# Two query blocks per TensorE step in the paired heads of block 1, and rounded products for the latents' sums of squares

## The reference

```
# block 1, per layer: differential attention (4 heads with two maps each) and
# dilated windows (8 heads of 64), causal, softmax over up to 512 keys
p = softmax(s); pd = p[:, :, 0] - lam * p[:, :, 1]; out = einsum(pd, v)
...
# block 2, per layer: sliding window, latent, stick-breaking and gated heads; the latent ones:
q = (_rmsnorm(cq, g_q) @ w_uq); kv = (_rmsnorm(ckv, g_kv) @ w_ukv)
```

## Time and profile before

| | |
|---|---|
| median of 3 runs | 2328.06 us (2327.0 to 2328.45) |
| the profiled execution's own time | 2326.94 us |
| its span, first to last instruction | 2325.2 us |
| TensorE busy | 2311.6 us (99%) |
| chain of work that ended last | 97% TensorE |
| granted TensorE clock | 0.999 of full speed |

### The profile page before, as it was taken

How to read it: one execution, slowest core, us unless ns; L and a number is a source line. 1 busy time by engine, 2 the same in 40 slices (tenths; PEclk the granted TensorE clock), 3 DMA queues, 4 the chain that set the end, 5 groups by cost and what they waited for, 6 DMA issues and landing times.

```text
span 2325.2 us, 30164 instructions
## 1 busy us (share of the span) xinstructions
PE 2311.6 (99%) x11444; PEld 1880.9 (81%) x11444; DVE 1478.5 (64%) x2773; ACT 981.3 (42%) x1825; POOL 0.2 (0%) x4
## 2 busy tenths in 40 slices
PE   9999999999999999999999999999999999999998
PEld 7888888888888888888877788888887768888887
DVE  6788764345578774344577668566566767668565
ACT  5356542223446653222567533133236664323222
POOL 0000000000000000000000000000000000000000
PEclk9999999999999999999999999999999999999999
DMA  5333333332343333333221232314303112422322
GB/s 176 106 107 105 99 104 91 100 95 96 91 116 105 105 93 116 100 98 111 65 87 55 64 129 91 127 59 140 126 29 97 55 46 100 145 82 90 130 70 91
DMA packets 73583, 226.32 MB, mean 97 GB/s; under 512 B 14240, under 2 KB 15136, under 8 KB 72672
## 3 DMA queue, kind: packets, MB, share of 16 engines
q1 hardware_dynamic: 73296, 224.13, 30.9%
q10 hardware_dynamic: 144, 0.26, 0.0%
HBM read 204.83 MB, written 2.10 MB: 89 GB/s over the span
## 4 chain that ended last, share of the span: by engine, by line
PE 97%; DVE 1%; ACT 1%; DMA 0%; issue 0%; DVEq 0%; SPq 0%
PE bank L585 26%; PE bank L587 25%; PE bank L586 25%; PE bank L2196 2%; PE bank L2194 2%; PE bank L2195 2%; PE bank L1279 2%; PE bank L2009 1%; PE bank L1968 1%; PE bank L1266 1%; PE bank L1993 1%; PE bank L519 1%; PE bank L1256 1%; PE bank L1254 1%; PE bank L2022 1%; PE bank L2051 0%
## 5 line engine op out<-in xcount | busy, mean ns | idle before, releaser
L585 PE MATMUL bank<-h_hi,w_hi 128*128 128x512 f32 x1984 | 788.1, 397 | 0.7 <-DVE w_lo L1125 0.2
L587 PE MATMUL bank<-h_lo,w_hi 128*128 128x512 f32 x1984 | 774.0, 390 | 0.0
L586 PE MATMUL bank<-h_hi,w_lo 128*128 128x512 f32 x1984 | 773.7, 390 | 0.0
L585 PEld LDWEIGHTS bank<-h_hi,w_hi 128*128 128x128 f32 x1984 | 372.9, 188 | 83.1 <-issue 10.4
L1125 DVE TENSOR_TENSOR w_lo<-raw_w,w_hi 128x1024 fp32r<-128x1024 f32 x314 | 379.1, 1222 | 93.1 <-ACT w_hi L1113 89.9
L587 PEld LDWEIGHTS bank<-h_lo,w_hi 128*128 128x128 f32 x1984 | 372.5, 188 | 79.3
L586 PEld LDWEIGHTS bank<-h_hi,w_lo 128*128 128x128 f32 x1984 | 373.2, 188 | 72.7 <-issue 1.2
L1113 ACT ACTIVATE w_hi<-raw_w 128x1024 fp32r<-128x1024 f32 x314 | 327.7, 1054 | 145.5 <-DMA raw_w<-w_dram 145.2
L2429 ACT ACTIVATE nrm<-bank 128x512 f32<-128x512 f32 x44 | 26.4, 599 | 289.5 <-PE bank L587 289.5
L1568 ACT ACTIVATE ext<-bank 128x512 f32<-128x512 f32 x48 | 28.7, 599 | 279.7 <-PE bank L587 279.7
L1868 DVE TENSOR_TENSOR rope_a<-ext,bank 128x512 f32<-128x512 f32 x32 | 22.0, 688 | 160.9 <-PE bank L587 107.4
(11 more groups left out here) (369 smaller groups left out, 3506.4 us busy)
## 6 DMA issues: line engine op xcount, KB each, us to landing
raw_w<-w_dram SPq DMA_DIRECT2D x312, 512.0 KB, 3.6
down_raw<-w_dram SPq DMA_DIRECT2D x36, 512.0 KB, 4.4
extra_raw<-w_dram SPq DMA_DIRECT2D x10, 512.0 KB, 4.5
k_lo<-k_lo SPq DMA_DIRECT2D x32, 128.0 KB, 2.4
ln_row<-row_dram SPq DMA_DIRECT2D x4, 1024.0 KB, 6.8
last_raw<-w_dram SPq DMA_DIRECT2D x8, 512.0 KB, 4.5
x<-x_dram SPq DMA_DIRECT2D x4, 512.0 KB, 6.4
rowp<-row_dram SPq DMA_DIRECT2D x2, 1024.0 KB, 9.8
```

What stands on the lines that cost most here:

```text
L585: nc.tensor.matmul(dst, lh, rh, start=start, stop=False)
L586: nc.tensor.matmul(dst, ll, rh, start=False, stop=False)
L587: return nc.tensor.matmul(dst, lh, rl, start=False, stop=stop)
```

## The change

- In the paired heads 4, 5 and 6 of block 1 (`JOINED1`) query blocks 0 and 1 are one TensorE step: their scores are issued together, into columns 0 to 127 and 128 to 383 of the two banks (`columns1`); then come the interlude of the steps before and the fills of both blocks. Their transposes and their weighted values are issued together too, one group and two groups later. ScalarE copies the transposed weights of both blocks at once (384 columns per map). VectorE and ScalarE still treat their softmax block by block.
- The read-out of the head before moves from qb 1 to qb 2 in joined heads, also the square of an output on ScalarE.
- In all heads the values' transposes go from qb 3 to qb 2 and the sum of squares from qb 2 to qb 3; the split of the squares goes from qb 1 to qb 2; the differential heads' epilogue goes behind the normalisation of qb 0.
- In block 2 the squares of both latents are split by VectorE into a high and a low part (`split_latent`), and TensorE sums them with two rounded products.
- In step 5 of block 2 ScalarE copies `kr` out ahead of the exponentials instead of behind them.

The diff's core (left out: the same change of columns, `columns1` for 0 to (qb+1) x 128, in `scores`, `pv`, `softmax_exp`, `row_max` and `normalise`, the waits that go with it, counts, and the removed lines of the old loop of TensorE, which is printed above):

```diff
+latent_sq = {"cq": (sq_lo, sb("cq_sq_lo", [P, SEQ], F32R, at=addr["sz0"])),
+             "ckv": (sq_lo, sb("ckv_sq_lo", [P, SEQ], F32R, at=addr["z_t"]))}
...
     if a < LAST:
-        LATE1[a, 3] = ("v", a + 1)
+        LATE1[a, 2] = ("v", a + 1)
     if 1 <= a <= N_A:
-        LATE1[a, 2] = ("sum", a - 1)
+        LATE1[a, 3] = ("sum", a - 1)
...
+JOINED1 = range(N_A, LAST)
+GROUPS1 = []
+for a in range(N_ATT):
+    GROUPS1 += [((a, 0), (a, 1))] if a in JOINED1 else [((a, 0),), ((a, 1),)]
+    GROUPS1 += [((a, 2),), ((a, 3),)]
+GROUP1_AT = {group[0]: i for i, group in enumerate(GROUPS1)}
+def second1(a, qb):
+    return qb == 1 and a in JOINED1
+def last1(a, qb):
+    return (a, 1) if qb == 0 and a in JOINED1 else (a, qb)
+def columns1(a, qb):
+    return slice(P, 3 * P) if second1(a, qb) else slice(0, (qb + 1) * P)
...
     def transposes(a, qb):
         pe.wait_ge(probs_normed, at(probs_normed, 4 * a + qb + 1))
         for m in range(1 if a < N_A else 2):
-            i = ti1(a, qb, m)
-            if i >= 2:
+            i, own = ti1(a, qb, m), columns1(a, qb)
+            to = own.start if a >= N_A else 0
+            if i >= 2 and not (a >= N_A and second1(a, qb)):
                 pe.wait_ge(t_out, at(t_out, i - 1))
             for b in range(qb + 1):
-                last = nc.tensor.transpose(T[i % 2][:, b * P:(b + 1) * P], pn[m][:, b * P:(b + 1) * P], ident)
+                last = nc.tensor.transpose(T[i % 2][:, to + b * P:to + (b + 1) * P],
+                                           pn[m][:, own.start + b * P:own.start + (b + 1) * P], ident)
             last.then_inc(t_ready, 1)
...
+    def late(a, qb):
+        use, f = LATE1.get((a, qb), (None, 0))
+        if use == "v":
+            v_transpose(f)
+        elif use == "sum":
+            sum_squares(f)
+    for i, group in enumerate(GROUPS1):
+        a, qb = group[0]
+        if qb == 0 and a in (0, LAST):
+            fill(a, qb, 0)
+        if banks1(a, qb) is S:
+            for own in group:
+                scores(*own)
+        if (a, qb) == (LAST, NB - 2):
+            scores(a, qb + 1)
+        if qb or a not in (0, LAST):
+            fill(a, qb, 0)
+        if i >= 2:
+            for own in GROUPS1[i - 2]:
+                pv(*own)
+        if i:
+            for own in GROUPS1[i - 1]:
+                transposes(*own)
+        fill(a, qb, 1)
+        late(a, qb)
+        for own in group[1:]:
+            fill(*own, 0)
+            fill(*own, 1)
+            late(*own)
...
     def pT_copy(a, qb):
+        together = a >= N_A and a in JOINED1 and qb == 0
+        width = columns1(*last1(a, qb)).stop if together else (qb + 1) * P
         for m in range(1 if a < N_A else 2):
             i = ti1(a, qb, m)
-            act.wait_ge(t_ready, at(t_ready, i + 1))
+            act.wait_ge(t_ready, at(t_ready, (ti1(a, 1, m) if together else i) + 1))
             w = 4 * a + qb - (1 if a < N_A else 0)
             if a == N_A and qb == 0:
                 w = 4 * a
             if w > 0:
                 act.wait_ge(pv_done, at(pv_done, w))
-            nc.scalar.activation(pT[i % 2][:, 0:(qb + 1) * P], T[i % 2][:, 0:(qb + 1) * P], ACT.Copy) \
-              .then_inc(t_out, 1)
+            nc.scalar.activation(pT[i % 2][:, 0:width], T[i % 2][:, 0:width], ACT.Copy) \
+              .then_inc(t_out, 2 if together else 1)
...
+            if before and not second1(a, qb):
+                for own in GROUPS1[GROUP1_AT[a, qb] - 1]:
+                    if not (own[0] >= N_A and second1(*own)):
+                        pT_copy(*own)
             if before:
-                pT_copy(*before)
                 if LATE1.get(before, ("", 0))[0] == "sum":
                     output_rstd(LATE1[before][1])
-            if qb == 1 and 1 <= a <= N_A:
+            if qb == (2 if a in JOINED1 else 1) and 1 <= a <= N_A:
                 output_squares(a - 1)
...
                 rotate(*ROTATE1[before])
-            if qb == 0 and 2 <= a < N_A + 2:
-                epilogue(a - 2)
-            elif qb == 1 and a > N_A:
+            if qb == (2 if a in JOINED1 else 1) and a > N_A:
                 epilogue(a - 1, False)
             elif qb == 3 and a > N_A:
                 split_y(8 + a - 1 - N_A)
                 dve.wait_ge(y_ready, at(y_ready, 4 + a))
             normalise(a, qb)
-            if qb == 1 and 1 <= a <= N_A:
+            if qb == 0 and 2 <= a < N_A + 2:
+                epilogue(a - 2)
+            if qb == 2 and 1 <= a <= N_A:
                 split_squares(a - 1)
...
-    def sum_squares(name, squares):
+    def sum_squares(name):
         pe.wait_ge(sq_ready, at(sq_ready, SQUARES[name]))
         r_free(name)
         bank = S[1] if name == "e7" else R
-        if name[0] == "e":
-            nc.tensor.matmul(bank[:, :], ones_r[:, :], sq_hi[:, :], start=True, stop=False)
-            last = nc.tensor.matmul(bank[:, :], ones_r[:, :], sq_lo[:, :], start=False, stop=True)
-        else:
-            last = nc.tensor.matmul(bank[:, :], ones_r[:, :].bitcast(F32), squares[:, :], start=True, stop=True)
-        last.then_inc(r_ready, 1)
+        high, low = latent_sq.get(name, (sq_hi, sq_lo))
+        nc.tensor.matmul(bank[:, :], ones_r[:, :], high[:, :], start=True, stop=False)
+        nc.tensor.matmul(bank[:, :], ones_r[:, :], low[:, :], start=False, stop=True).then_inc(r_ready, 1)
...
         if step == FILL_FIRST:
             tiles_out(ENDS[step, 0])
+        if "kr" in ENDS[step, 0]:
+            tile_copy("kr")
...
         if step != FILL_FIRST:
-            tiles_out([name for name in ENDS[step, 0] if name not in ("uk0", "uv0")])
+            tiles_out([name for name in ENDS[step, 0] if name not in ("kr", "uk0", "uv0")])
...
     high_step, sum_step = [0, 0], [0, 0]
+    def split_latent(name, squares):
+        high, low = latent_sq[name]
+        st.wait(st(nc.vector.tensor_copy(high[:, :], squares[:, :])))
+        nc.vector.tensor_tensor(low[:, :], squares[:, :], high[:, :].bitcast(F32), ALU.subtract).then_inc(sq_ready, 1)
     def add_squares(name, a, b):
         dve.wait_ge(sq_parts, at(sq_parts, TWO_SQUARES[name]))
-        nc.vector.tensor_tensor(a[:, :], a[:, :], b[:, :], ALU.add).then_inc(sq_ready, 1)
+        st.wait(st(nc.vector.tensor_tensor(a[:, :], a[:, :], b[:, :], ALU.add)))
+        split_latent(name, a)
...
+        if late == "ckv":
+            dve.wait_ge(sq_parts, at(sq_parts, TWO_SQUARES["ckv"]))
+            split_latent("ckv", z_t)
         if LATE.get(step - 2) == "cq":
             query_latents(1)
```

More of the change, by code:

```diff
@@ L1250, in scores @@
                         pe.wait_ge(tile_out[t], at(tile_out[t], before1(B1_GATE)))
+                own = columns1(a, qb)
                 for m in range(2):
-                    if u and bank is S:
+                    if u and bank is S and not second1(a, qb):
                         pe.wait_ge(max_ready, at(max_ready, u - 1 + m))
-                    nc.tensor.matmul(bank[m][:, 0:nk], q_two[i][m][:, block_q], k_two[i][m][:, 0:nk], start=True, stop=False)
+                    nc.tensor.matmul(bank[m][:, own], q_two[i][m][:, block_q], k_two[i][m][:, 0:nk], start=True, stop=False)
                 for m in range(2):
-                    nc.tensor.matmul(bank[m][:, 0:nk], q_two[i][m][:, block_q], k_lo[i][m][:, 0:nk], start=False, stop=True) \
+                    nc.tensor.matmul(bank[m][:, own], q_two[i][m][:, block_q], k_lo[i][m][:, 0:nk], start=False, stop=True) \
                       .then_inc(scores_ready, 1)
@@ L1276, in pv @@
                     if b == 0:
-                        pe.wait_ge(t_out, at(t_out, ti1(a, qb, m) + 1))
+                        copied = ti1(*last1(a, qb), 1) if a >= N_A and a in JOINED1 and qb < 2 else ti1(a, qb, m)
+                        pe.wait_ge(t_out, at(t_out, copied + 1))
+                    of = columns1(a, qb).start if a >= N_A else 0
                     rows = slice(0, P) if a < N_A else slice(HD * m, HD * m + HD)
                     last = nc.tensor.matmul(O[rows, cols], vs[a % 2][:, b, rows],
-                                            pT[ti1(a, qb, m) % 2][:, b * P:(b + 1) * P],
+                                            pT[ti1(a, qb, m) % 2][:, of + b * P:of + (b + 1) * P],
                                             start=(b == 0), stop=(b == qb))
@@ L1323, in tensor_block1 @@
                 tile1(n, 1)
[L1325 to L1345, removed]
+            def late(a, qb):
[27 more added lines that the diff above has]
+                    late(*own)
+                gate_early(NB * a + qb)
             pv(LAST, NB - 2)
@@ L1509, in softmax_exp @@
             def softmax_exp(a, qb, m):
[L1510 removed]
+                u, own = 8 * a + 2 * qb + m, columns1(a, qb)
                 act.wait_ge(max_ready, at(max_ready, u + 1))
[L1512 removed]
+                nc.scalar.activation(prob[m][:, own], prob[m][:, own], ACT.Exp, scale=-1.0,
                                      bias=small[:, 24 + 2 * qb + m:25 + 2 * qb + m],
```

(6 more changed lines are left out.)

30 lines of the change are left out of this document (13 added, 17 removed).

## The result

The changed kernel takes **2330.18 us** (median of 20 runs, 2329.14 to 2331.15) where the kernel before takes 2327.11 in the same comparison (20 runs, 2326.34 to 2328.45). The ratio is 1.0013, with a 95% interval of 1.0007 to 1.0019: 3.1 us slower. The forecast was 5.0 us faster, so about 8 us are missing. (The forecast's base of 2328.06 was the median of three runs, 1.0 above the median of these twenty. Counted from 2327.11, 5.0 us faster would be 2322.1.) The profiled execution took 2330.43 us, its span 2328.6, and its granted clock is 0.999 of full speed, as before; the clock has no part in this.

What follows compares the result with a forecast made beforehand. The prediction took TensorE's stream, busy for 99% of the span, to bound the kernel. Its terms, 1.6 + 1.5 + 1.8 = 5.0 us with second decimals, gave 2323.0 us from a median of 2328.06, range 2321.2 to 2325.8.

Steps and rivals of the forecast that it cites:

- What bounds the kernel: Whole kernel: TensorE is busy for 99% of the span, so a microsecond counts only if it leaves TensorE's stream.
- Term A: Block 2, latents' sums of squares: two rounded products save 0.41 us a sum, four times, 1.6 us.
- Term B: Block 2, step 5: copying kr earlier removes TensorE's wait for its bank, 0.76 us in each layer, 1.5 us.
- Term C: Block 1, joined query blocks: one interlude fewer per joined head saves 0.30 us a pair, six pairs, 1.8 us.
- What the moves trigger: Block 1: moved read-out, value transposes, sums and epilogue make TensorE wait nowhere; costed at nothing.
- The slower one: Block 1, joined heads: read-out ahead of block 2's normalisation makes TensorE wait at transposes; 2336 us, chance 0.03.
- The rivals with less from B or from C: Step 5's wait stays or changes hands, 2324.5 us, chance 0.18; interludes give nothing, 2325.0 us, chance 0.12.
- The third, more than was counted: Joined pairs give 0.4 us each, plus small distances at half tiles: 5.6 to 6.2 us, 2322.0 us, chance 0.14.
- The sum: Whole kernel: 1.6 + 1.5 + 1.8 = 5.0 us saved with the second decimals, giving 2323.0 us.

Runs made afterwards that it cites:

- e1: The changed kernel with block 1 and the copy of kr as in the kernel before, leaving only the latents' sums changed: 2327.32 us, ratio 1.0.
- e11: The kernel before with only the copy of kr put ahead of the exponentials of step 5: 2325.86 us, ratio 0.9994.
- e2: The changed kernel with all of block 2's edits (sums and copy of kr), block 1 as in the kernel before: 2323.55 us, ratio 0.9984.
- e4: The changed kernel with one table load in each root of block 1 in place of two: 2322.18 us, ratio 0.9979.
- e8: The changed kernel with one table load in the root and without the joining of query blocks: 2323.97 us, ratio 0.9987.
- e10: The changed kernel with a third table load in each root, between Ln and Exp: 2340.63 us, ratio 1.0057.

## Why the prediction was wrong

- **What bounds the kernel: right.** Only TensorE's stream counts. It also means that waits of 0.5 to 0.9 us, twelve of them, on an engine that is busy for 99% decided the sign.
- **Term A, 0.41 a sum: right in size**, the two products take 0.46 for 0.87, and the margins on VectorE held. But it is no term of its own: alone it gave nothing (e1). It counts only with B.
- **Term B: right, and the bank's holder rightly read** against the profile's attribution in the earlier trace rows: with the copy moved the gap goes (e11), and in e1 the profile names the copy. A and B were put at 3.1 together and measured 3.4 (e2).
- **Term C, 0.30 a pair: right in kind, somewhat small.** The joining gives 1.1 us a layer by the tile products and 0.38 in head 6. The 1.8 us between the medians (e4 against e8), just what was forecast, is luck: they hold a loss at the late weight unit, 0.7 us in e4's profile, of which the prediction says nothing. By the rule of the Trainium skill that is quoted there, that back to back only the columns count, it would have been 0; the runs disagree with it.
- **The step that failed is "What the moves trigger".** It said that the swapped places "keep one step between maker and user" and that the epilogue "uses time in which VectorE would idle", and costed both at nothing. The maker is not the sum but the root behind it on ScalarE, and between root and epilogue the step that was there is gone. I had not looked up the root in ScalarE's rows, where two loads of 1.28 us stand ahead of its two operations. A wait was added to VectorE's queue, and I didn't ask what was behind it: the row maxima and normalisations of two query blocks. VectorE idles 3.6 to 3.9 us for the root in each of heads 2 to 5, and TensorE then waits for the normalisations. It costs 8.0 us (changed kernel against e4) and scales one for one from there (e10).
- **The rivals.** The slower one had the right kind (VectorE late at transposes) at the wrong place: the read-out ahead of block 2 in the joined heads. Head 6 shows that margin held. The rivals with less from B or from C didn't come true. The third, more than was counted, did as far as the terms go: 3.4 us in block 2 and 2.2 from the joining are 5.6, where the forecast had 5.0.
- **The sum.** 5.6 gained, 7.9 lost to the late roots and 0.8 to the late weight unit make 3.1 lost, as measured. Without the late roots 5.6 less 0.7 is 4.9, and e4 gives 4.8. That this is within 0.2 of the forecast's 5.0 is in part luck: terms that were a little small cover a second loss that was left out.

Open is why that weight unit comes later in the joined kernels. No run was made for it.

## What to carry to other kernels

When a change moves the maker of a value, follow the value to its last hand: here product, then root on another engine, then reader, and look up the duration of each in that engine's own rows, table loads included. Then ask what is queued behind the reader, since an engine that works in order passes the wait on to work that has nothing to do with it. And terms in one stream aren't independent: time saved ahead of a wait comes back only if the wait is moved too.

## What the runs showed of the hardware

Ln and Exp in sequence cost two table loads of 1.28 us, 3.8 us for a root of 1.2 us of arithmetic, in all eight roots; asking for the set that holds both by name takes one load off the root and moves it ahead of the next Tanh. The load has no cost beside its 1.28 us in these traces (gaps of 0.01 and 0.02 us around it, and 1.3 us more on TensorE for one load more in e10).
